# Ten chunks of the convolution's input product in 512- and 256-column multiplications: a two-block transformer kernel on one core

## The chip, the core and the metric

The kernel is one program on one core of a Trainium2 chip. The metric is device time in microseconds (us) for one execution, and the median of several executions counts. Everything is computed from float32 inputs in HBM, and the output is float32.

## The reference, cut to what matters

The reference runs a first model of two layers (short convolution mixer, SwiGLU, dilated attention, SwiGLU) and a hybrid layer behind it, on 256 tokens of width 1024. The change lies in the mixer of the very first layer:

```python
def short_conv_mixer(x, w_in, conv_w, w_out):
    b_gate, c_gate, h = jnp.split(x @ w_in, 3, axis=-1)
    u = c_gate * h
    conv = ...   # depthwise, causal, 3 taps over the tokens: sum over tap of u[t + tap - 2] * conv_w[tap]
    return (b_gate * conv) @ w_out
```

`x` is the RMS-normalised input (256 x 1024), `w_in` is 1024 x 3072, `w_out` is 1024 x 1024.

## The kernel before

**Precision.** Every large product is made of three: a float32 matrix is held as a high part rounded to fp32r and a low part, the rest. The product is high x high + high weights x low input + low weights x high input, all summed in PSUM.

**Chunks.** The weights of all stages come in one sequence of chunks, numbered from the start of the program; a chunk of the stage `conv_in` is 1024 x 256 weights (1 MB, in two halves). `conv_in` has chunks 0 to 11, and `conv_out` chunks 12 to 15. A chunk passes four hands:
- SyncE's queue issues the two loads into `raw` (L583). There are `raw` buffers for two chunks, so the loads of chunk n wait until the low parts of chunk n - 2 are made (`lo_ready`).
- ScalarE copies each half to `w_hi` (L1372), three chunks ahead of the chunk that TensorE is on.
- VectorE subtracts and writes each half to `w_lo` (L1877), two chunks ahead.
- TensorE multiplies. It starts a chunk when both halves of `w_lo` are there (`ready`). `w_hi` and `w_lo` have four slots.

**The product of a chunk.** `feature_major` (L666) makes two output blocks of 128 features x 256 tokens, in one PSUM bank. Each of the 8 k-tiles takes three multiplications of 256 columns: L681 (high weights, high input), L682 (high weights, low input) and L683 (low weights, high input). That is 48 a chunk. Chunk 0 has its own form, and chunk 1 has two short pieces of other work in its middle (`row_and_vectors`).

**What happens with the products.** Chunks come in threes, i = l // 3: first `c_gate`, then `h`, then `b_gate` for 256 features; r = l % 3 tells which. For r = 0 ScalarE copies the bank to `gate` (L1737). For r = 1 VectorE makes `up` = bank x `gate` (L2331), multiplies by the tokens' squared norm factor (L2334, signal `up_set`), and runs the three taps into `cv`: the middle one that all begins with as a scaled copy (L2338, twice), the other two as multiply-adds (L2343, four times), then the norm factor (L2348). For r = 2 VectorE makes `mid` = bank x `cv` (L2358), ScalarE copies it to `a_hi` (L1745) and GpSimd makes `a_lo` (L2514), which `conv_out` reads.

**Order.** Every engine runs an order written by hand, and an engine does its instructions strictly in that order. On VectorE the body for chunk l is: first the low parts of chunk l + 2, then the work on the product of chunk l. At l = 3 it also copies constants out of PSUM and computes the rotary angles (L2351, L1978 to L1990). On ScalarE the body for l is: the high parts of chunk l + 3, then the copy for r = 0, then `a_hi` for r = 2.

The up stage behind already multiplies in another form, `gated_blocks` (L824): `x_hi` and `x_lo` lie side by side in one tile `x_both`, so one multiplication of 512 columns gives high weights x both inputs, and a second of 256 columns adds low weights x high input to the first half. The bank's two halves must then be summed outside TensorE: ScalarE copies the second half out, VectorE adds the first.

Of the kernel before, what the change touches and what calls it, by code (L numbers as in the profile page):

```python
# [25 lines left out]
ALU = mybir.AluOpType  # L26
# [6 lines left out]
T = 256  # L33
# [64 lines left out]
def build(nc, a, out):  # L98
# [4 lines left out]
    with ctx:  # L103
# [173 lines left out]
        by_name = {}  # L277
# [46 lines left out]
        logits_low, logits_set = sem("logits_low"), sem("logits_set")  # L324
        mid_ready = sem("mid_ready")
# [92 lines left out]
        GATE_BANK = (2, 0)  # L418
        NORM_OF = {"up0": 1, "up1": 3}
# [238 lines left out]
        def _(pe):  # L658
# [463 lines left out]
            def emit(ph):  # L1122
                name = ph.name
                if name == "conv_in":
                    for l in range(ph.count):
                        if l > 0:
                            ready(ph, l % 4, l // 4)
                        if l == 0:
                            feature_major_first(ph, 0, x_hi, x_lo, 0)
                        else:  # L1130
                            feature_major(ph, l % 4, x_hi, x_lo, middle=row_and_vectors if l == 1 else None)
# [69 lines left out]
                elif name in ("conv_out", "w_out2"):  # L1201
# [4 lines left out]
                    if name == "conv_out":  # L1206
                        tokens(ph, 0, 0, range(4), bank[0][0], hi, lo, first=True, tile=tile)
# [154 lines left out]
        def _(act):  # L1362
# [364 lines left out]
            def emit(ph):  # L1727
                name = ph.name
                if name == "conv_in":
                    for l in range(ph.count):  # L1730
                        i, r, s = l // 3, l % 3, (ph.n0 + l) % 4
                        ahead(ph, l % 4, l // 4, split, 3)
                        if r == 0:
                            act.wait_ge(product_done, l + 1)
                            if i >= 2:
                                wait_emptied(act, ph, (l - 5) % 4, (l - 5) // 4)
                            nc.scalar.activation(flat2(gate[:, i % 2]), ps[:, s, :], ACT.Copy)\  # L1737
                                .then_inc(emptied[s], 1)
# [4 lines left out]
                        if r == 2:  # L1743
                            wait_emptied(act, ph, l % 4, l // 4)
# [120 lines left out]
        def _(dve):  # L1865
# [451 lines left out]
            def emit(ph):  # L2317
                name = ph.name
                if name == "conv_in":
                    for l in range(ph.count):  # L2320
                        i, r, s = l // 3, l % 3, (ph.n0 + l) % 4
                        ahead(ph, l % 4, l // 4, split, 2)
                        if l == 1:
                            set_row(0)
                            link(nc.vector.tensor_tensor(r_sq[:], rstd[:], rstd[:], ALU.mult))
                        if r == 1:
                            wait_emptied(dve, ph, (l - 1) % 4, (l - 1) // 4)
                            dve.wait_ge(product_done, l + 1)
                            if i == 0:
                                dve.wait_ge(zeroed, 1)  # L2330
                            nc.vector.tensor_tensor(up[:, :, 2:], ps[:, s, :].rearrange("p (m t) -> p m t", m=2),  # L2331
                                                    gate[:, i % 2], ALU.mult).then_inc(emptied[s], 1)
                            wait_emptied(dve, ph, l % 4, l // 4)
# [298 lines left out]
```

## Time and profile before

| | us |
|---|---|
| median of 3 runs | 1077.6 (1077.33 to 1078.9) |
| the profiled execution | 1076.97 |
| its span, first to last instruction | 1074.9 |
| TensorE busy in the span | 1066.9 |
| VectorE busy | 808.1 |
| ScalarE busy | 650.5 |
| GpSimd busy | 55.0 |

The 2.1 us between the execution's time and its span lie before the first and after the last instruction. Matmuls are pipelined: the record of one matmul is longer than the distance to the next one's start, so the distance between starts tells what a row of them costs. A view of a stretch lists groups of like instructions with start, length and count; two independent instructions of VectorE or ScalarE overlap a little at their ends.

### The profile page before, as it was taken

How to read it: one execution, taken by the hardware profiler on the slowest of the kernel's cores; microseconds unless marked ns; L12 is line 12 of the kernel's file. 1: busy time of each engine (PE TensorE's matmuls, PEld its weight loads, DVE VectorE, ACT ScalarE, POOL GpSimd, SP SyncE). 2: the span in 40 equal slices, each digit the busy share in tenths (PEclk: the TensorE clock that was granted, in tenths of full speed). 3: DMA queues.
4: the chain of work that ended last, by engine and by line, in shares of the span. 5: the costliest groups of instructions: out<-in, count | busy, mean ns of one | idle time of the engine just before them, and what ended most of it. 6: DMA issues, size and time to landing. Idle time of an engine off the chain costs nothing.

```text
span 1074.9 us, 19326 instructions
## 1 busy us (share of the span) xinstructions
PE 1066.9 (99%) x7328; PEld 964.1 (90%) x7328; DVE 808.1 (75%) x1227; ACT 650.5 (61%) x982; POOL 55.0 (5%) x47
## 2 busy tenths in 40 slices
PE   8999999999999999999999999999999999999998
PEld 8998888888898999999889888889998989999987
DVE  5986777874588787887878778636797878888960
ACT  6446746564588777777676465535465757656650
POOL 0010000000000000000000000000200111222300
PEclk9999999999999999999999999999999999999999
DMA  8565665678285776552347658753445664565660
GB/s 265 167 206 185 198 214 175 223 250 249 60 236 171 195 193 185 166 160 80 134 146 223 209 164 267 269 158 99 137 135 157 219 206 134 182 194 180 232 235 20
DMA packets 219788, 195.63 MB, mean 182 GB/s; under 512 B 9881, under 2 KB 195277, under 8 KB 219725
## 3 DMA queue, kind: packets, MB, share of 16 engines
q1 hardware_dynamic: 219369, 194.55, 58.1%
q8 instruction: 42, 0.69, 0.3%
q10 hardware_dynamic: 356, 0.22, 0.1%
q14 instruction: 21, 0.17, 0.0%
HBM read 191.85 MB, written 1.05 MB: 179 GB/s over the span
## 4 chain that ended last, share of the span: by engine, by line
PE 90%; DVE 5%; ACT 2%; DMA 1%; issue 1%; SPq 0%; DVEq 0%; ACTq 0%
PE ps L835 24%; PE ps L906 9%; PE ps L736 8%; PE ps L738 8%; PE ps L737 8%; PE ps L681 6%; PE ps L683 6%; PE ps L682 6%; DVE w_lo L1877 2%; PE ps L850 2%; PE ps L849 2%; PE ps L848 2%; DMA raw<-in_conv_w_in 1%; ACT w_hi L1372 1%; PE ps L784 1%; PE ps L750 1%
## 5 line engine op out<-in xcount | busy, mean ns | idle before, releaser
L1877 DVE TENSOR_TENSOR w_lo<-raw,w_hi 128x1024 fp32r<-128x1024 f32 (+1 forms) x298 | 398.2, 1379 | 55.2 <-ACT w_hi L1372 54.2
L1372 ACT ACTIVATE w_hi<-raw 128x1024 fp32r<-128x1024 f32 (+1 forms) x298 | 331.6, 1156 | 117.3 <-PE ps L738 38.2
L835 PE MATMUL ps<-x_both,w_hi 128*128 128x512 f32 x736 | 173.3, 391 | 0.1
L835 PEld LDWEIGHTS ps<-x_both,w_hi 128*128 128x128 f32 x736 | 136.2, 188 | 29.5 <-issue 1.2
L681 PE MATMUL ps<-x_both,w_hi 128*128 128x256 f32 x560 | 159.3, 284 | 0.6 <-DVE w_lo L1877 0.6
L683 PE MATMUL ps<-x_both,w_lo 128*128 128x256 f32 x560 | 158.5, 283 | 0.0
L682 PE MATMUL ps<-x_both,w_hi 128*128 128x256 f32 x560 | 158.5, 283 | 0.0
L736 PE MATMUL ps<-w_hi,a_hi 128*128 128x512 f32 x296 | 115.7, 391 | 0.0
L738 PE MATMUL ps<-w_hi,a_lo 128*128 128x512 f32 x296 | 115.2, 389 | 0.0
L737 PE MATMUL ps<-w_lo,a_hi 128*128 128x512 f32 x296 | 115.2, 389 | 0.0
L681 PEld LDWEIGHTS ps<-x_both,w_hi 128*128 128x128 f32 x560 | 107.5, 192 | 1.4 <-DVE w_lo L1877 1.0
L682 PEld LDWEIGHTS ps<-x_both,w_hi 128*128 128x128 f32 x560 | 107.5, 192 | 0.0
L683 PEld LDWEIGHTS ps<-x_both,w_lo 128*128 128x128 f32 x560 | 107.5, 192 | 0.0
L835 PEld LDWEIGHTS ps<-x_both,w_lo 128*128 128x128 f32 x736 | 91.8, 192 | 2.0
L835 PE MATMUL ps<-x_both,w_lo 128*128 128x256 f32 x736 | 92.8, 283 | 0.0
L1509 ACT ACTIVATE gu<-ps 128x512 f32<-128x512 f32 x20 | 12.0, 598 | 89.2 <-PE ps L835 89.2
L738 PEld LDWEIGHTS ps<-w_hi,a_lo 128*128 128x128 f32 x296 | 55.6, 188 | 11.6
L737 PEld LDWEIGHTS ps<-w_lo,a_hi 128*128 128x128 f32 x296 | 55.6, 188 | 11.3
L736 PEld LDWEIGHTS ps<-w_hi,a_hi 128*128 128x128 f32 x296 | 55.6, 188 | 11.2
L1610 ACT ACTIVATE rot_x<-rot_s 32x512 f32<-32x512 f32 x84 | 52.9, 630 | 16.3 <-DVE rot_s L2123 15.6
L848 PE MATMUL ps<-w_hi,x_both 128*128 128x384 f32 x168 | 56.3, 335 | 0.0
L850 PE MATMUL ps<-w_hi,x_both 128*128 128x384 f32 x168 | 56.2, 335 | 0.0
(263 smaller groups left out, 1698.0 us busy)
## 6 DMA issues: line engine op xcount, KB each, us to landing
raw<-in_ffn_w_gate_up SPq DMA_DIRECT2D x80, 512.0 KB, 5.2
raw<-in_w_up SPq DMA_DIRECT2D x44, 512.0 KB, 4.5
raw<-in_ffn_w_down SPq DMA_DIRECT2D x24, 768.0 KB, 5.9
raw<-in_conv_w_in SPq DMA_DIRECT2D x24, 512.0 KB, 4.9
raw<-in_w_q SPq DMA_DIRECT2D x48, 256.0 KB, 4.7
raw<-in_w_kv SPq DMA_DIRECT2D x48, 256.0 KB, 4.3
raw_v<-in_w_kv SPq DMA_DIRECT2D x48, 256.0 KB, 3.9
raw<-in_w_in SPq DMA_DIRECT2D x20, 512.0 KB, 4.9
```

Of the source, the lines that this page charges most:

```text
L681: nc.tensor.matmul(o, wh[:, k0 + k, c], hi[:, k, :], start=(k == 0), stop=False)
L682: nc.tensor.matmul(o, wh[:, k0 + k, c], low, start=False, stop=False)
L683: ins = nc.tensor.matmul(o, wl[:, k0 + k, c], hi[:, k, :], start=False, stop=(k == kt - 1))
L736: nc.tensor.matmul(o, high, wh[:, k, :], start=(first and k == ks[0]), **flags)
L737: nc.tensor.matmul(o, high, wl[:, k, :], start=False, **flags)
L738: ins = nc.tensor.matmul(o, low, wh[:, k, :], start=False, **flags)
L835: ins = nc.tensor.matmul(o_, w[:, k, c], x, start=(k == 0 and part == int(low_first)), stop=(k == KD - 1), skip_group_check=True)
L848: nc.tensor.matmul(o, high, wh[:, k, :], start=(k == 0), stop=False)
L850: ins = nc.tensor.matmul(o, low, wh[:, k, :], start=False, stop=(k == KD - 1))
L906: ins = nc.tensor.matmul(o_, w[:, k, c], x, start=(k == 0 and part == int(low_first)), stop=(k == KD - 1), skip_group_check=True)
L1372: nc.scalar.activation(w_hi[:, s, a * ph.cols:b * ph.cols], src, ACT.Copy)\
L1877: nc.vector.tensor_tensor(w_lo[:, s, c], src, w_hi[:, s, c], ALU.subtract)\
```

## The change

In `conv_in`, from chunk 2 on:
- TensorE uses `gated_blocks`: 16 multiplications of 512 columns and 16 of 256 a chunk in place of 48 of 256. The two blocks take two PSUM banks; four pairs of banks are used in turn (`CONV_BANK`). In odd chunks the low weights go first. There are extra waits before chunks 2, 3 and 5 and before `conv_out` for the banks.
- ScalarE now first waits for the product of chunk l, copies the second halves of its two banks to `gate`, `up` or `mid` (a 128 x 512 copy, ten of them; three took the place of the copies for r = 0, L1737), and only then makes the high parts of chunk l + 3.
- VectorE adds the first halves in place (ten sums), and for r = 1 and r = 2 the multiplication by `gate` or `cv` comes as an instruction of its own behind the sum, from SBUF.
- In all four threes ScalarE makes the middle tap from `up` (two instructions of 128 x 256) behind the high parts of chunk l + 3; VectorE waits for it (`tap_base`) before the other taps.

```diff
@@ TensorE
-                            feature_major(ph, l % 4, x_hi, x_lo, middle=row_and_vectors if l == 1 else None)
+                            gated_blocks(ph, l % 4, (0, 1), CONV_BANK[l % 4], low_first=(l % 2 == 1)).then_inc(product_done, 1)
@@ ScalarE
-                        ahead(ph, l % 4, l // 4, split, 3)
-                        if r == 0:
+                        if l < 2:
+                            ahead(ph, l % 4, l // 4, split, 3)
+                        if l != 1:
                             act.wait_ge(product_done, l + 1)
...
+                        elif l > 1:
...
+                            dst = (gate[:, i % 2], up[:, :, 2:], mid[:, i % 2])[r]
+                            bank = CONV_BANK[l % 4]
+                            nc.scalar.activation(dst, ps[:, bank:bank + 2, T:2 * T], ACT.Copy).then_inc(conv_low, 1)
+                            ahead(ph, l % 4, l // 4, split, 3)
+                        if r == 1:
+                            act.wait_ge(up_set, i + 1)
+                            for m in range(2):
+                                ins = nc.scalar.activation(cv[:, m, :], up[:, m, 2:], ACT.Identity,
+                                                           scale=v("conv_w", 16 + 2 * i + m))
+                            ins.then_inc(tap_base, 1)
@@ VectorE
+                        if l > 1:
+                            dst = (gate[:, i % 2], up[:, :, 2:], mid[:, i % 2])[r]
+                            bank = CONV_BANK[l % 4]
+                            dve.wait_ge(conv_low, l - 1)
+                            nc.vector.tensor_tensor(dst, ps[:, bank:bank + 2, 0:T], dst, ALU.add).then_inc(emptied[s], 1)
                         if r == 1:
...
+                                link(nc.vector.tensor_tensor(up[:, :, 2:], up[:, :, 2:], gate[:, i % 2], ALU.mult))
                             nc.vector.tensor_tensor(up[:, :, 2:], up[:, :, 2:], by_token(r_sq), ALU.mult)\
                                 .then_inc(up_set, 1)
                             dve.wait_ge(up_set, i + 1)
-                            for m in range(2):
-                                ins = nc.vector.tensor_scalar(cv[:, m, :], up[:, m, 2:], v("conv_w", 16 + 2 * i + m),
-                                                              None, ALU.mult)
-                            link(ins)
+                            dve.wait_ge(tap_base, i + 1)
...
                         if r == 2:
...
-                            nc.vector.tensor_tensor(flat2(mid[:, i % 2]), ps[:, s, :], flat2(cv[:]), ALU.mult)\
-                                .then_inc(emptied[s], 1)
+                            wait_emptied(dve, ph, l % 4, l // 4)
+                            nc.vector.tensor_tensor(mid[:, i % 2], mid[:, i % 2], cv[:], ALU.mult).then_inc(conv_mixed, 1)
```

On VectorE, the work for l = 4 and the start of l = 5, in the kernel before (`hi_ready` is ScalarE's signal for a high half, `v_seq` VectorE's own, `emptied` and `product_done` those of the banks and of TensorE):

```order
L1877 TENSOR_TENSOR w_lo<-raw,w_hi 128x1024 [waits hi_ready] x2
L2331 TENSOR_TENSOR up<-ps,gate 128x2x256 [waits product_done,emptied3]
L2334 TENSOR_TENSOR up<-up,r_sq 128x2x256 [waits emptied0]
L2338 TENSOR_SCALAR cv<-up,vec 128x256 [waits up_set]
L2338 TENSOR_SCALAR cv<-up,vec 128x256
L2343 SCALAR_TENSOR_TENSOR cv<-up,vec,cv 128x256 [waits v_seq]
```

The same place in the changed kernel:

```order
L1906 TENSOR_TENSOR w_lo<-raw,w_hi 128x1024 [waits hi_ready] x2
L2359 TENSOR_TENSOR up<-ps,up 128x2x256 [waits conv_low]
L2370 TENSOR_TENSOR up<-up,gate 128x2x256 [waits emptied0,emptied3]
L2371 TENSOR_TENSOR up<-up,r_sq 128x2x256 [waits v_seq]
L2377 SCALAR_TENSOR_TENSOR cv<-up,vec,cv 128x256 [waits tap_base,up_set]
```

A sum stands ahead of the multiplication by `gate`, and the two scaled copies are gone, with a wait for ScalarE in their place.

On ScalarE, l = 2 to l = 4 in the kernel before:

```order
L1372 ACTIVATE w_hi<-raw 128x1024 [waits product_done,raw_in2]
L1372 ACTIVATE w_hi<-raw 128x1024 [waits raw_in3]
L1745 ACTIVATE a_hi<-mid 128x512 [waits emptied2]
L1372 ACTIVATE w_hi<-raw 128x1024 [waits product_done,raw_in0]
L1372 ACTIVATE w_hi<-raw 128x1024 [waits raw_in1]
L1737 ACTIVATE gate<-ps 128x512 [waits product_done]
```

The changed kernel, from the copy for l = 3 to the one for l = 5:

```order
L1760 ACTIVATE gate<-ps 128x512 [waits product_done]
L1385 ACTIVATE w_hi<-raw 128x1024 [waits product_done,raw_in0]
L1385 ACTIVATE w_hi<-raw 128x1024 [waits raw_in1]
L1760 ACTIVATE up<-ps 128x2x256 [waits conv_mixed,product_done]
L1385 ACTIVATE w_hi<-raw 128x1024 [waits product_done,raw_in2]
L1385 ACTIVATE w_hi<-raw 128x1024 [waits raw_in3]
L1765 ACTIVATE cv<-up,vec 128x256 [waits up_set]
L1765 ACTIVATE cv<-up,vec 128x256
L1760 ACTIVATE mid<-ps 128x512 [waits product_done]
```

The copy of a product now stands ahead of the high parts of the chunk three further on, and the two instructions of the middle tap stand behind those high parts, which wait for the loads (`raw_in`).

## Rows read from the trace of the kernel before

**Rows 1.** The page: engines' busy time and share, granted TensorE clock in 40 slices.
```profile
PE 1066.9 (99%) x7328; PEld 964.1 (90%) x7328; DVE 808.1 (75%) x1227; ACT 650.5 (61%) x982; POOL 55.0 (5%) x47
PEclk9999999999999999999999999999999999999999
```

**Rows 2.** TensorE's waits, whole span: for whom, us in total, times, longest.
```profile
PE ps L698 <- ACT w_hi L1372: 1.5, 1, 1.5
...
PE ps L681 <- DVE w_lo L1877: 0.6, 2, 0.4
```

**Rows 3.** Busy us of PE, PEld, DVE, ACT, POOL (and clock, DMA) in two stretches.
```profile
24.90:51.60 26.70, 26.40 (x221) 26.20 (x219) 25.84 (x44) 12.35 (x14) 1.53 (x1) 1.00 0.51 162
51.60:80.60 29.00, 28.89 (x240) 28.89 (x241) 24.03 (x32) 14.04 (x17) 3.61 (x2) 1.00 0.65 210
```

**Rows 4.** The chain that ended last, 20 to 82 us: start, us, what.
```profile
23.50 1.07 ACT w_hi L1372
24.59 1.23 DVE w_lo L1877
...
31.30 2.36 DVE w_lo L1877 x2
...
34.27 3.36 DVE w_lo L1877 x2
...
49.30 2.37 DVE w_lo L1877 x2
```

**Rows 5.** TensorE's timeline, first matmuls of chunk 7 and of chunk 12.
```profile
51.71 0.39 PE L681 MATMUL ps<-x_both,w_hi 128*128 128x256 f32 x1 [0.41 <-DVE w_lo L1877]
...
80.61 0.40 PE L736 MATMUL ps<-w_hi,a_hi 128*128 128x512 f32 x1
```

**Rows 6.** TensorE's timeline in the up stage, where `gated_blocks` already runs.
```profile
146.59 7.44 PE L835 MATMUL ps<-x_both,w_hi 128*128 128x512 f32 x32
153.87 4.00 PE L835 MATMUL ps<-x_both,w_lo 128*128 128x256 f32 x32
157.71 7.44 PE L835 MATMUL ps<-x_both,w_hi 128*128 128x512 f32 x32
```

**Rows 7.** VectorE's timeline, l = 4 to l = 6.
```profile
44.65 0.68 DVE L2331 TENSOR_TENSOR up<-ps,gate 128x512 f32<-128x512 f32 x1
45.37 0.69 DVE L2334 TENSOR_TENSOR up<-up,r_sq 128x512 f32<-128x512 f32 x1
46.09 0.62 DVE L2338 TENSOR_SCALAR cv<-up,vec 128x256 f32<-128x256 f32 x2
46.74 1.80 DVE L2343 SCALAR_TENSOR_TENSOR cv<-up,vec,cv 128x256 f32<-128x256 f32 x4
...
51.58 0.68 DVE L2358 TENSOR_TENSOR mid<-ps,cv 128x512 f32<-128x512 f32 x1
52.18 2.35 DVE L1877 TENSOR_TENSOR w_lo<-raw,w_hi 128x1024 fp32r<-128x1024 f32 x2
```

**Rows 8.** VectorE's groups in the up stage: busy, mean ns, idle before.
```profile
L2016 DVE TENSOR_TENSOR gu<-gu,rstd 128x512 f32<-128x512 f32 x20 | 13.8, 692 | 0.7
...
L2014 DVE TENSOR_TENSOR gu<-ps,gu 128x512 f32<-128x512 f32 x20 | 13.8, 691 | 40.1 <-ACT gu L1509 40.1
```

**Rows 9.** ScalarE's timeline: 128x256 instructions with a column as scale, bias, or both.
```profile
6.29 1.57 ACT L1387 ACTIVATE x_both<-ps,vec 128x256 fp32r<-128x256 f32 x4 [2.44 <-DVE vec L1965]
...
845.94 1.69 ACT L1724 ACTIVATE gates<-gates,vec 128x256 f32<-128x256 f32 x4
...
949.64 1.10 ACT L1563 ACTIVATE gate<-scaled,vec 128x256 f32<-128x256 f32 x2 [2.24 <-DVE scaled L2062]
```

**Rows 10.** ScalarE's second high half of chunk 10, VectorE's second low half of chunk 9.
```profile
60.41 1.06 ACT L1372 ACTIVATE w_hi<-raw 128x1024 fp32r<-128x1024 f32 x1 [0.32 <-DMA raw<-in_conv_w_in]
...
57.67 1.22 DVE L1877 TENSOR_TENSOR w_lo<-raw,w_hi 128x1024 fp32r<-128x1024 f32 x1 [0.90 <-ACT w_hi L1372]
```

**Rows 11.** The page's DMA issues: count, size, median us from issue to landing.
```profile
raw<-in_conv_w_in SPq DMA_DIRECT2D x24, 512.0 KB, 4.9
```

More of the change, by code:

```diff
@@ L1127, in emit @@
                             ready(ph, l % 4, l // 4)
+                        if l == 2:
+                            pe.wait_ge(vec_set, 1)
+                        elif l == 3:
+                            wait_emptied(pe, ph, 0, 0)
+                            wait_emptied(pe, ph, 1, 0)
+                        elif l == 5:
+                            pe.wait_ge(vec_set, 2)
                         if l == 0:
                             feature_major_first(ph, 0, x_hi, x_lo, 0)
+                        elif l == 1:
+                            feature_major(ph, l % 4, x_hi, x_lo, middle=row_and_vectors)
                         else:
-                            feature_major(ph, l % 4, x_hi, x_lo, middle=row_and_vectors if l == 1 else None)
+                            gated_blocks(ph, l % 4, (0, 1), CONV_BANK[l % 4], low_first=(l % 2 == 1)).then_inc(product_done, 1)
                 elif name in ("up0", "up1"):
@@ L1206, in emit @@
                     if name == "conv_out":
+                        wait_emptied(pe, by_name["conv_in"], 1, 2)
+                        wait_emptied(pe, by_name["conv_in"], 0, 2)
                         tokens(ph, 0, 0, range(4), bank[0][0], hi, lo, first=True, tile=tile)
@@ L1731, in emit @@
                         i, r, s = l // 3, l % 3, (ph.n0 + l) % 4
-                        ahead(ph, l % 4, l // 4, split, 3)
-                        if r == 0:
+                        if l < 2:
+                            ahead(ph, l % 4, l // 4, split, 3)
+                        if l != 1:
                             act.wait_ge(product_done, l + 1)
-                            if i >= 2:
-                                wait_emptied(act, ph, (l - 5) % 4, (l - 5) // 4)
-                            nc.scalar.activation(flat2(gate[:, i % 2]), ps[:, s, :], ACT.Copy)\
-                                .then_inc(emptied[s], 1)
+                        if l == 0:
+                            nc.scalar.activation(flat2(gate[:, 0]), ps[:, s, :], ACT.Copy).then_inc(emptied[s], 1)
+                        elif l > 1:
+                            if r == 0 and i >= 2:
+                                act.wait_ge(up_set, i - 1)
+                            elif r == 1:
+                                act.wait_ge(conv_mixed, i)
+                            elif r == 2 and i >= 2:
+                                act.wait_ge(mid_split, i - 1)
+                            dst = (gate[:, i % 2], up[:, :, 2:], mid[:, i % 2])[r]
[8 more added lines that the diff above has]
+                            ins.then_inc(tap_base, 1)
                         if l == 5:
```

18 lines of the change are left out of this document (9 added, 9 removed).

## The prediction

> **What bounds the kernel now.** I read the page first. TensorE is busy 1066.9 us, 99% of the span, and the granted clock is full in all 40 slices [rows 1]. What the kernel gains or loses is therefore read from TensorE's own pace and from its few waits. The waits come next. Behind its first chunk TensorE stands still almost nowhere: 0.6 us in all for VectorE's low parts in `conv_in` [rows 2]. This would say that VectorE, with 75% of the span, has room. The stretches say otherwise: from 24.9 to 51.6 us VectorE is busy 25.84 of 26.7 us, while TensorE is busy for nearly all of it too [rows 3]. Both engines are full there, side by side. The chain shows which of them leads: from 24.6 us on it runs through VectorE alone, by way of the low parts of chunks 4 and 5, the angles and the taps, up to the low parts of chunk 7 (49.30, 2.37 us long) [rows 4]. TensorE takes them up at 51.71 after 0.41 us of standing still [rows 5]. After that point VectorE is ahead: busy 24.03 of 29.0 us from 51.6 on [rows 3], and TensorE runs chunks 7 to 11 without a stop until 80.61 [rows 5].
>
> So there are two places. Until chunk 7 begins, VectorE's order sets the time, and a faster TensorE only waits longer. From chunk 7 to chunk 11 TensorE sets it.
>
> **TensorE's part.** Before, five chunks take 80.61 - 51.71 = 28.90 us, 5.78 each [rows 5]. The new form stands in the up stage: 32 multiplications of 512 columns take 153.87 - 146.59 = 7.28 us from start to start, 32 of 256 take 157.71 - 153.87 = 3.84 us, so two chunks take 11.12 and one 5.56 us [rows 6]. The change gives 0.22 us a chunk. All ten chunks would give 2.2 us, but only the five from chunk 7 on lie where TensorE sets the time: 5 x 0.22 = **1.10 us gained**. The five before it (2 to 6) only make TensorE arrive 1.1 us earlier at a chunk whose low parts aren't there. The loads have no part in this: ten chunks are the same bytes as before.
>
> **VectorE's part, up to the low parts of chunk 7.** Everything here is in the line that TensorE waits for, since VectorE has 0.9 us of idle time in 26.7 [rows 3].
> - A 128 x 512 sum with one operand in PSUM took 691 ns, a multiplication with both in SBUF 692 [rows 8]. From start to start such an instruction takes 45.37 - 44.65 = 0.72 us where the next one needs its result, and 52.18 - 51.58 = 0.60 where it doesn't [rows 7]. I take these.
> - l = 2: the sum for `mid` with the multiplication behind it, where one instruction stood: +0.72. l = 3: the sum for `gate`: +0.60. l = 4: the sum for `up`: +0.72.
> - The middle tap at l = 1 and l = 4 leaves VectorE, where it took 46.74 - 46.09 = 0.65 us [rows 7]. But nothing is there to fill its place: `up` must be ready before, the other taps need it, and VectorE works in order. ScalarE's pair has no like in the trace. Four instructions of that size from PSUM took 1.57 us, half of which is 0.79; four from SBUF with one column operand took 1.69, half of which is 0.85; a pair from SBUF with two column operands took 1.10 [rows 9]. The second of these has the same source and the same number of columns. A pair overlaps only once where four overlap three times, so I take 0.90. With 0.03 us for the way to the other engine (24.59 against 23.50 + 1.07 in [rows 4]), twice, VectorE stands for 0.96 us in place of 0.65: +0.31, and from +0.2 to +0.5 by the other rows. Twice: **+0.62**.
> - Sum: 0.72 + 0.60 + 0.72 + 0.62 = **2.66 us**, between 2.2 (0.60 for each sum, +0.2 for each tap) and 3.1.
>
> What VectorE waits for must be there. At l = 1 `up` is ready near 28.1 (31.30 - 2.56 for the taps - 0.65), and ScalarE has the tap and the copy of product 2 to do from there, while VectorE comes to that copy at 31.30 + 2.36 = 33.7 [rows 4]. At l = 4 ScalarE must be through with chunk 7's high parts when `up` is ready, at 46.09 + 0.72 + 0.60 + 0.72 + 0.31 = 48.4 [rows 7]. It is busy 12.35 of 26.7 us in this stretch [rows 3], and VectorE's line before has no gap for a high part. The seven more copies of ScalarE cost nothing here for the same reason. GpSimd's first `a_lo` (1.53 us in [rows 3]) lies beside the low parts of chunk 5, which took 3.36 us in place of 2.36 [rows 4]; it moves with them and adds nothing new.
>
> Chunk 7 then begins at 51.71 + 2.66 = 54.37, and `conv_out` at 54.37 + 5 x 5.56 = 82.17, against 80.61: **+1.56 us**.
>
> The Trainium skill (VectorE: DVE Perf Modes, "The TRN2 errata — SBUF-src ops pay a fixed extra latency per instruction") lists 58 cycles of fixed cost for VectorE with its source in SBUF and 120 with it in PSUM. By that table the two multiplications of the line that now read SBUF alone would each be about 0.065 us shorter (an estimate from the page), and the sum 1.43 in place of 1.56. The rows show 692 and 691 ns, no difference, and I keep 1.56.
>
> **Behind chunk 7.** The delay must not grow. The thin place is l = 7. The low parts of chunk 8 were done at 52.18 + 2.35 = 54.5 [rows 7]; they come 2.66 + 0.72 later, at 57.9, since the multiplication of l = 5 waits for its sum too. ScalarE's second high half of chunk 10 ended at 60.41 + 1.06 = 61.47, having waited for its load [rows 10], and the load waits for those low parts. It moves by 3.4 to 64.9, and the middle tap stands behind it on ScalarE: done near 65.8. VectorE would have wanted it at about 63.65 (chunk 9's low parts at 57.67 + 1.22 + 2.66 = 61.5, and three instructions of 0.72, [rows 10]). The other taps take 49.30 - 46.74 = 2.56 [rows 4, 7], chunk 10's low parts 2.3: done at 70.7. TensorE wants chunk 10 at 54.37 + 3 x 5.56 = 71.05. That is 0.4 us of room, and if GpSimd's second `a_lo` costs chunk 8's low parts the 1.0 us that the first one cost, the room is gone and 0.6 us are lost. I take 0.2 for it. Chunk 13 repeats this at l = 10 with the same kind of wait, with some 0.5 us of room.
>
> The sum is +1.56 + 0.2 = **+1.8 us**. On the profiled execution that is 1076.97 + 1.8 = 1078.8. That execution is 0.6 below the median of the runs, and the prediction is for the median: 1077.6 + 1.8 = **1079.4**.
>
> **Rivals.**
> 1. **ScalarE's order becomes the bound a second time (slower).** Place: the tap at l = 7 and l = 10, behind high parts that wait for loads. For it: 0.4 us of room. Against it: that load came 60.41 - 54.5 = 5.9 us after its release, where the median is 4.9 [rows 11]; at the median the room is 1.4 us. It decides when the second high half of chunk 10 ends later than 65.3. Each us later goes whole into the end. With the GpSimd overlap (0.6) and one us more between l = 7 and l = 10: 1.56 + 1.6 = +3.2, 1080.8; with both places bad, +5.
> 2. **TensorE keeps its whole gain (faster).** This needs that VectorE's line wasn't what held chunk 7. Then 10 x 0.22 = 2.2 us and the 0.4 of standing still are the most to be had: 1075.2. The 25.84 of 26.7 us speak against it. Halfway, with VectorE's line 2.2 us longer, it is 2.2 - 1.10 = +1.1, 1078.7, which is still my forecast's case.
> 3. **The clock falls.** TensorE will stand still for about 0.5, 1.2 and 2.4 us before chunks 5, 6 and 7. The longest stop in the trace is 1.5 us [rows 2], and the granted clock stayed at full, 2.4 GHz [rows 1]. No row here is at the lower level. At half the pace each chunk costs 5.6 us more, so one chunk gives 1079.4 + 5.6 = 1085. The Trainium skill (TensorE: Matmul & The Clock Gate, "Part 1: The HAM clock gate") says that an idle TensorE is put back to 1.2 GHz. No run here shows a stop long enough to test it.
>
> **How the numbers follow.** Forecast, VectorE's line lengthened by 2.2 to 3.1 us and little lost behind (+1.0 to +2.4): 0.55. Rival 1 (+2.4 to +5): 0.29. Rival 2: 0.05. Rival 3: 0.03. Less lengthened than I sum, for a reason that I don't see (-1 to +1.0): 0.08. A measurement of this kernel tells 0.2% from no change, 2.15 us: faster is below 1075.4, slower above 1079.8. The forecast lies close to the upper bound, so a fifth of it goes to slower: 0.11 + 0.29 + 0.03, less a little of rival 1 near the bound, makes 0.42; faster 0.05; same 0.53. The range is 1077.4 to 1082.2: below it lie rival 2 and part of the unseen, above it rival 3 and the end of rival 1.
>
> **What would show it.** In the changed trace: 512- and 256-column matmuls at 0.2275 and 0.12 us from start to start, 5.56 us a chunk. TensorE's waits for low parts at chunks 5 to 7 near 4 us in sum, against 0.6. The low parts of chunk 7 done near 54.2, VectorE without idle time before but for two gaps of some 0.96 us ahead of the taps. `conv_out` beginning near 82.2 to 82.4. From there to the end every stage with its old length. Wrong would be: chunk 7 starting before 53.9 or after 54.9, a gap ahead of the taps that is over 2.5 us at l = 7, a wait of TensorE at chunks 10 or 13 over 0.6 us, or a lower granted clock.

## The result, and the profile after

The changed kernel takes 1080.59 us (median of 17 runs, 1078.11 to 1081.59), the kernel before 1077.6 on the same chip (17 runs). The ratio is 1.0024, 95% interval 1.0018 to 1.0031: 2.6 to 3.0 us slower. The forecast was 1079.4 with a range of 1077.4 to 1082.2, a chance of 0.53 for no difference that can be told and 0.42 for slower by over 0.2%. The range holds the time, and the less likely of the two came. The forecast itself is 1.2 us too low. In the profiled execution one thing explains what it missed, and a second profile, further down, shows that it isn't the only one.

The profiled execution took 1080.59 us, its span is 1078.2. Its page beside [rows 1]:

```profile
PE 1068.5 (99%) x7168; PEld 959.5 (89%) x7168; DVE 813.1 (75%) x1229; ACT 657.0 (61%) x997; POOL 54.5 (5%) x47
...
PEclk8999999999999999999999999999999999999999
```

There are 160 matmuls fewer, as the change says (ten chunks, 32 in place of 48), and VectorE and ScalarE have more to do. The first slice is not at full clock any more. TensorE's waits, beside [rows 2] (for whom, us in total, times, longest):

```profile
PE ps L873 <- DMA h<-in_x: 2.1, 2, 1.9
...
PE ps L837 <- DVE w_lo L1906: 1.8, 1, 1.8
```

The wait for low parts is 1.8 us, where it was 0.6, and it is one single stop. TensorE's timeline from chunk 2 to `conv_out`, beside [rows 5] (start, length, line, form, count, in brackets the standing still before it):

```profile
24.77 3.82 PE L837 MATMUL ps<-x_both,w_hi 128*128 128x512 f32 x16
...
54.57 2.74 PE L837 MATMUL ps<-x_both,w_lo 128*128 128x256 f32 x16 [1.84 <-DVE w_lo L1906]
57.11 8.48 PE L837 MATMUL ps<-x_both,w_hi 128*128 128x512 f32 x32
65.43 4.00 PE L837 MATMUL ps<-x_both,w_lo 128*128 128x256 f32 x32
...
84.03 0.39 PE L738 MATMUL ps<-w_hi,a_hi 128*128 128x512 f32 x1
```

Chunk 7 begins at 54.57 (forecast 54.37), `conv_out` at 84.03 (forecast 82.2 to 82.4; before 80.61). From `conv_out` to the end of the span it is 1078.2 - 84.03 = 994.2 us, before 1074.9 - 80.61 = 994.3. So the whole loss lies ahead of `conv_out`: 3.42 us, of which 54.57 - 51.71 = 2.86 are there when chunk 7 begins, and 0.56 come behind it. That second part should have been a gain of 1.1. From start to start, the 16 multiplications of 256 columns at 54.57 take 2.54 us and not 1.92, and the 32 of 512 behind them 8.32 and not 7.28. Together they take 1.66 us too long, and 1.66 - 1.10 = 0.56. Why, the stretches show, beside [rows 3] (busy time of PE, PEld, DVE, ACT, POOL, then the granted clock, DMA share and GB/s):

```profile
0.00:20.00 20.00, 16.23 (x94) 15.11 (x95) 8.75 (x16) 11.95 (x21) 0.51 (x6) 0.83 0.81 257
...
52.00:56.00 4.00, 2.15 (x18) 1.95 (x17) 3.93 (x6) 2.40 (x5) 0.00 (x0) 0.99 0.36 95
56.00:59.00 3.00, 3.00 (x12) 2.61 (x11) 3.00 (x2) 2.05 (x3) 1.54 (x1) 0.50 0.89 268
59.00:61.00 2.00, 2.00 (x10) 1.60 (x9) 2.00 (x4) 1.06 (x1) 0.00 (x0) 0.92 0.79 224
```

TensorE stood still for 1.84 us, worked again from 54.57 on, and from 56 to about 59.3 us it was granted 0.50, which is 1.2 in place of 2.4 GHz. That is some 3.3 us at half the pace, which accounts for the 1.66 us. The first 20 us are at 0.83 too. There TensorE had stood still for 1.9 us for the input's load (L873). Whether that made the clock fall isn't shown: in the trace of the filled stop, further down, it stood still for 1.49 and 1.51 us within the first 12 us and stayed at full clock. This earlier fall cost next to nothing here, since until chunk 7 VectorE sets the time, and its first `up` begins at 26.53, where it began at 26.64 before.

VectorE's line, beside [rows 7], and ScalarE's pair for the tap at l = 4:

```profile
46.24 0.68 DVE L2359 TENSOR_TENSOR up<-ps,up 128x512 f32<-128x512 f32 x1
47.03 0.69 DVE L2370 TENSOR_TENSOR up<-up,gate 128x512 f32<-128x512 f32 x1
47.76 0.69 DVE L2371 TENSOR_TENSOR up<-up,r_sq 128x512 f32<-128x512 f32 x1
49.51 1.89 DVE L2377 SCALAR_TENSOR_TENSOR cv<-up,vec,cv 128x256 f32<-128x256 f32 x4 [1.06 <-ACT cv L1765]
51.42 0.69 DVE L2382 TENSOR_TENSOR cv<-cv,rstd 128x512 f32<-128x512 f32 x1
52.15 2.36 DVE L1906 TENSOR_TENSOR w_lo<-raw,w_hi 128x1024 fp32r<-128x1024 f32 x2
54.43 0.68 DVE L2359 TENSOR_TENSOR mid<-ps,mid 128x512 f32<-128x512 f32 x1
```

```profile
48.48 0.91 ACT L1765 ACTIVATE cv<-up,vec 128x256 f32<-128x256 f32 x2 [4.34 <-DVE up L2371]
```

I measure this line from the start of the first `up` (l = 1) to the instruction behind the low parts of chunk 7. That is a length on one engine, so an early or late start of the program doesn't enter. Before it is 51.58 - 26.64 = 24.94 us, after it is 54.43 - 26.53 = 27.90: **+2.96**, forecast +2.66.

### The profile page after: what moved, and what is told of

The parts are those of the page before. It is cut to its first block, busy times and chain, and to the rows that moved or that the text cites. A ratio compares the mean times of both kernels' runs of the same rounds, so it can differ in the third digit from the quotient of the medians.

```text
span 1078.2 us, 19030 instructions
## 1 busy us (share of the span) xinstructions
PE 1068.5 (99%) x7168; PEld 959.5 (89%) x7168; DVE 813.1 (75%) x1229; ACT 657.0 (61%) x997; POOL 54.5 (5%) x47
## 3 DMA queue, kind: packets, MB, share of 16 engines
HBM read 191.85 MB, written 1.05 MB: 179 GB/s over the span
## 4 chain that ended last, share of the span: by engine, by line
PE 88%; DVE 6%; ACT 2%; DMA 2%; SPq 1%; issue 1%; DVEq 0%; ACTq 0%
PE ps L837 27%; PE ps L908 9%; PE ps L738 8%; PE ps L739 8%; PE ps L740 8%; PE ps L683 5%; PE ps L685 5%; PE ps L684 5%; DVE w_lo L1906 3%; PE ps L852 2%; PE ps L851 2%; PE ps L850 2%; DMA raw<-in_conv_w_in 1%; ACT w_hi L1385 1%; PE ps L951 1%
## 5 line engine op out<-in xcount | busy, mean ns | idle before, releaser
L837 PE MATMUL ps<-x_both,w_hi 128*128 128x512 f32 x896 | 211.5, 392 | 0.0
L837 PEld LDWEIGHTS ps<-x_both,w_hi 128*128 128x128 f32 x896 | 166.8, 189 | 35.2 <-DVE w_lo L1906 0.7
L837 PEld LDWEIGHTS ps<-x_both,w_lo 128*128 128x128 f32 x896 | 112.2, 192 | 4.5 <-DVE w_lo L1906 2.0
L837 PE MATMUL ps<-x_both,w_lo 128*128 128x256 f32 x896 | 113.6, 284 | 1.8 <-DVE w_lo L1906 1.8
L683 PE MATMUL ps<-x_both,w_hi 128*128 128x256 f32 x400 | 113.8, 284 | 0.0
L685 PE MATMUL ps<-x_both,w_lo 128*128 128x256 f32 x400 | 113.2, 283 | 0.0
L684 PE MATMUL ps<-x_both,w_hi 128*128 128x256 f32 x400 | 113.2, 283 | 0.0
L683 PEld LDWEIGHTS ps<-x_both,w_hi 128*128 128x128 f32 x400 | 76.8, 192 | 0.3 <-issue 0.3
L684 PEld LDWEIGHTS ps<-x_both,w_hi 128*128 128x128 f32 x400 | 76.8, 192 | 0.0
L685 PEld LDWEIGHTS ps<-x_both,w_lo 128*128 128x128 f32 x400 | 76.7, 192 | 0.0
```

What stands on the lines that cost most here:

```text
L683: nc.tensor.matmul(o, wh[:, k0 + k, c], hi[:, k, :], start=(k == 0), stop=False)
L684: nc.tensor.matmul(o, wh[:, k0 + k, c], low, start=False, stop=False)
L685: ins = nc.tensor.matmul(o, wl[:, k0 + k, c], hi[:, k, :], start=False, stop=(k == kt - 1))
L837: ins = nc.tensor.matmul(o_, w[:, k, c], x, start=(k == 0 and part == int(low_first)), stop=(k == KD - 1), skip_group_check=True)
```

## Experiments

**The theory**: VectorE's line up to chunk 7 is longer by the three sums and the two taps, and its end decides when TensorE takes up chunk 7. Behind that, the new form gains 1.1 us; and the stop before chunk 7 sometimes lets the clock fall, which costs about 1.6 us. **Rivals**: the low clock comes from something else (the late load, chance) and the stop has no part in it; the loss is from ScalarE's new order; the angles alone are what makes chunk 7 late, so that elsewhere VectorE has room.

### The tap put back

```diff
@@ ScalarE
-                        if r == 1:
-                            act.wait_ge(up_set, i + 1)
-                            for m in range(2):
-                                ins = nc.scalar.activation(cv[:, m, :], up[:, m, 2:], ACT.Identity,
-                                                           scale=v("conv_w", 16 + 2 * i + m))
-                            ins.then_inc(tap_base, 1)
@@ VectorE
-                            dve.wait_ge(tap_base, i + 1)
+                            for m in range(2):
+                                ins = nc.vector.tensor_scalar(cv[:, m, :], up[:, m, 2:], v("conv_w", 16 + 2 * i + m),
+                                                              None, ALU.mult)
+                            link(ins)
```

> The changed kernel with the middle tap back on VectorE. Theory A: the two gaps ahead of the taps (1.74 and 1.75 us from the start of the multiplication by r_sq to the first tap, against 1.38 and 1.37 before) go, chunk 7 begins 0.75 us earlier, near 53.8: 1080.6 - 0.75 = 1079.8 if the clock still falls, 1078.4 if a stop of 1.1 us no longer lets it fall. If the move to ScalarE relieved VectorE, as a count of busy time says (0.6 us an instance), it would be slower, 1081.8.

1079.16 us against 1077.08 for the kernel before, ratio 1.0014 (1.0005 to 1.0024). The line is 53.65 - 26.57 = 27.08 us: 2.14 of the 2.96 are the sums, and 0.82 are the two taps. The stops stay:

```profile
46.06 3.96 PE L837 MATMUL ps<-x_both,w_hi 128*128 128x512 f32 x16 [0.72 <-DVE w_lo L1900]
...
53.79 2.17 PE L837 MATMUL ps<-x_both,w_lo 128*128 128x256 f32 x16 [1.86 <-DVE w_lo L1900]
```

In this execution the clock stayed full behind a stop of 1.86 us. So such a stop doesn't lower it each time. The other executions have both of the cases that were expected: the 4 with a mean clock of 1.00 have a median of 1077.94 (expected 1078.4), the 7 below it 1079.58 (expected 1079.8). In those 7 no trace shows where the clock fell.

### The tap moved alone

The kernel before, with nothing but the middle tap on ScalarE (the lines of the diff above, the other way round).

> The kernel before with the middle tap on ScalarE and nothing else. Theory A: VectorE stands 0.37 to 0.41 us longer at each tap than its own two instructions took, so the line up to chunk 7 is 25.7 us in place of 24.94 and the time rises by 0.75. If the offload frees VectorE, the line shortens by up to 1.2 us and the 0.4 us stop goes: 0.4 faster.

The line is 52.97 - 27.30 = 25.67 us, +0.73. The two gaps ahead of the taps:

```profile
29.77 1.79 DVE L2347 SCALAR_TENSOR_TENSOR cv<-up,vec,cv 128x256 f32<-128x256 f32 x4 [1.05 <-ACT cv L1743]
...
48.14 1.80 DVE L2347 SCALAR_TENSOR_TENSOR cv<-up,vec,cv 128x256 f32<-128x256 f32 x4 [1.06 <-ACT cv L1743]
```

VectorE stands for 1.05 us in place of working 0.65. The time is 1077.86 against 1077.43, ratio 1.0003 (0.9994 to 1.0011), which alone is no difference that can be told. In executions at full clock it is 1077.85 (10 runs) against 1077.20 (26 runs), +0.65, and with so few runs that isn't clear of noise either. What is shown is the line: taking work off VectorE made it longer.

### The sums cut short

```diff
-                            nc.vector.tensor_tensor(dst, ps[:, bank:bank + 2, 0:T], dst, ALU.add).then_inc(emptied[s], 1)
+                            w = 8 if l < 5 else T
+                            nc.vector.tensor_tensor(dst[:, :, 0:w], ps[:, bank:bank + 2, 0:w], dst[:, :, 0:w], ALU.add)\
+                                .then_inc(emptied[s], 1)
```

The sums for l = 2 to 4 are made for 8 of 256 tokens only; the rest of these products lacks its first half.

> The changed kernel with VectorE's sums at l = 2, 3 and 4 made for 8 of 256 columns only, so part of the convolution's input product is left incomplete. Theory A: each sum still costs its start, 0.15 to 0.25 us of 0.60 to 0.79, so the line up to chunk 7 is about 1.5 us shorter than the changed kernel's 27.9, near 26.4, and chunk 7 begins 1.5 us earlier: 1.2 to 1.5 us under the changed kernel's median with a full clock, and 2 to 3 under its median if the shorter stop (0.3 us) no longer lets the clock fall: near 1077.9. Rival D: no effect.

The time is 1078.85 against 1077.43, ratio 1.0016 (1.0007 to 1.0025), 0.9 above what was expected. The short sums take 0.17 us each, but the line is 53.25 - 25.94 = 27.31 us, only 0.59 less than the changed kernel's. Two things of opposite sign are in this. From start to start the three sums take 0.20, 0.08 and 0.27 us in place of 0.72, 0.60 and 0.79, which is 1.56 less, as expected. But at l = 1 VectorE waited 2.00 us for the tap and not 1.04, which is 0.96 more: ScalarE's high part ahead of the tap had waited for its load. TensorE now stops in three places:

```profile
34.33 3.93 PE L837 MATMUL ps<-x_both,w_hi 128*128 128x512 f32 x16 [0.58 <-DVE w_lo L1906]
...
53.39 2.18 PE L837 MATMUL ps<-x_both,w_lo 128*128 128x256 f32 x16 [1.85 <-DVE w_lo L1906]
...
71.36 3.92 PE L837 MATMUL ps<-x_both,w_hi 128*128 128x512 f32 x16 [1.03 <-DVE w_lo L1906]
```

The last one, before chunk 10, is a new place, and it is the place of the prediction's rival 1. The load for ScalarE's second high part of chunk 10 came late, the tap stands behind that high part, and VectorE waited 3.37 us for it at l = 7:

```profile
64.43 1.06 ACT L1385 ACTIVATE w_hi<-raw 128x1024 fp32r<-128x1024 f32 x1 [3.13 <-DMA raw<-in_conv_w_in]
...
66.39 1.80 DVE L2379 SCALAR_TENSOR_TENSOR cv<-up,vec,cv 128x256 f32<-128x256 f32 x4 [3.37 <-ACT cv L1765]
```

### The angles later

```diff
@@ VectorE (angles() stood under l == 3; its last five instructions are angles_end)
+                        if l == 6:
                             angles()
+                        if l == 9:
+                            angles_end()
```

ScalarE's two table instructions move from l = 5 to l = 10 with it.

> The changed kernel with the rotary angles (4.5 us of VectorE, 39.47 to 43.97 in its trace) moved from l = 3 to l = 6 and l = 9, and ScalarE's sine and cosine from l = 5 to l = 10. Theory A (VectorE's line up to chunk 7 sets the time): chunk 7's low parts come at 49.9 in place of 54.4, TensorE no longer stops in front of it, the ten chunks give their whole 2.2 us and the 0.4 us of the old stop: near 1075.1, and conv_out begins some 5.5 us earlier than in the changed kernel when the start is alike. Theory B (the clock falls because TensorE stops in front of chunk 7): the granted clock stays full from 50 us on. Rival C (the fall of the clock belongs to the new form of multiplication or to the program's start, not to the stop): a stretch at 0.5 is still there between 50 and 62 us. Rival D (the new form costs time somewhere else): stays above 1077.6.

A miss. It takes 1078.04 against 1077.08, ratio 1.0009 (1.0000 to 1.0018), and 1075.1 was expected. The line up to chunk 7 is 4.25 us shorter (51.29 - 27.64 = 23.65). But the stops only went elsewhere:

```profile
35.08 3.93 PE L837 MATMUL ps<-x_both,w_hi 128*128 128x512 f32 x16 [0.79 <-DVE w_lo L1906]
69.96 3.92 PE L837 MATMUL ps<-x_both,w_hi 128*128 128x512 f32 x16 [1.11 <-DVE w_lo L1906]
87.27 0.50 PE L738 MATMUL ps<-w_hi,a_hi 128*128 128x512 f32 x1 [0.47 <-DVE w_lo L1906]
```

And over the whole stage:

```profile
27.00:81.00 54.00, 52.09 (x302) 45.54 (x301) 49.19 (x68) 30.49 (x40) 4.65 (x3) 1.00 0.56 175
```

VectorE is busy for 49.19 of 54.0 us, and three gaps ahead of the taps (1.05, 1.39, 1.06) are another 3.5. That leaves 1.3 us. With the sums and the handed-over taps VectorE has next to no room anywhere in `conv_in`, and where the angles stand decides in which chunk that is seen. "The angles alone make chunk 7 late" falls.

The half of the forecast that is about the clock held: no stop is longer than 1.11 us, the clock is full in the whole stage, and no execution has a mean below 0.997. The four that have 0.997 take 1078.18, the other seven 1078.04.

### The new form from chunk 7 on only

Chunks 2 to 6 as before; chunks 7 to 11 in the new form, with the tap on VectorE.

```diff
@@ TensorE
+                        elif l < 7:
+                            feature_major(ph, l % 4, x_hi, x_lo, bank=4 if l == 5 else None)
                         else:
                             gated_blocks(ph, l % 4, (0, 1), CONV_BANK[l % 4], low_first=(l % 2 == 1)).then_inc(product_done, 1)
@@ VectorE
-                        if l > 1:
+                        if l >= 7:
```

A first form of it left chunk 5 in its old bank, which is one of the pair that chunk 7 takes.

> The new form of multiplication, the copies and the sums only from chunk 7 on, chunks 2 to 6 and the middle tap as in the kernel before. Theory A: VectorE's line up to chunk 7 is that of the kernel before, so the stop there stays at 0.4 us and conv_out begins 1.1 us earlier than before: 1076.5, clock full. Rival D (the new form costs time where it stands): not faster than 1077.6.

1076.97 against 1077.08, ratio 0.9999 (0.9990 to 1.0008). The mistake shows as a stop before chunk 7:

```profile
53.29 2.14 PE L837 MATMUL ps<-x_both,w_lo 128*128 128x256 f32 x16 [1.27 <-DVE mid L2396]
```

With chunk 5 in bank 4, which is the form of the diff:

> As e3_from_seven, but chunk 5 keeps its old form in bank 4, so that chunk 7 (banks 0 and 1) needn't wait for VectorE's work on chunk 5; in e3_from_seven that wait was 1.27 us in place of 0.4. Theory A: chunk 7 begins right behind its low parts, line from the first up to the low parts of chunk 7 24.95 us as before, TensorE gains 5 x 0.22: 1.1 us under the kernel before, 0.9 under e3_from_seven. Rival D (the new form itself costs time): no better than e3_from_seven.

1076.25 against 1077.43, ratio 0.9989 (0.9980 to 0.9997): 1.2 us faster, where five chunks at 0.22 make 1.1. In the trace the five chunks take 27.80 us (52.36 to 80.16), 5.56 each. VectorE's line keeps its old length, 50.48 - 25.53 = 24.95. So the gain behind chunk 7 is real and of the size forecast, and it is the sums and taps ahead of chunk 7 that cost.

### The form from chunk 4 on, with the angles later

Both halves of what was learned: the old form for chunks 2 and 3, the new one from 4 on, the tap on VectorE, and the angles at l = 6 and l = 9.

> New form from chunk 4 on, middle tap on VectorE, rotary angles at l = 6 and l = 9, sine and cosine at l = 10. Theory A: up to chunk 7 VectorE gives away 4.5 us of angles and takes on 2.0 us of sums, so its line is 2.4 us shorter than before and TensorE stops nowhere in front of chunks 5 to 13: eight chunks give 1.8 us and the old stop, where it stands, up to 0.4: 1.8 to 2.2 us under the kernel before. If VectorE is full again behind chunk 7 (sums and angles, 3.4 + 4.5 us against 5.0 of idle time), TensorE stops in front of chunk 10 or 13 and the gain is 1 us or less.

**1075.91** against 1077.4, ratio 0.9985 (0.9976 to 0.9994). At full clock it is 1075.07 (6 runs) against 1077.34 (17 runs), 2.3 us less. The two engines side by side, and the one wait for low parts that is left:

```profile
27.00:78.00 51.00, 51.00 (x315) 46.03 (x314) 48.94 (x70) 27.14 (x33) 4.64 (x3) 1.00 0.56 177
```

```profile
PE ps L683 <- DVE w_lo L1910: 0.2, 1, 0.2
```

TensorE is busy for all of 51 us, and VectorE still has 2 us. Eight chunks at 0.22 are 1.8, and the old standing still before chunk 7 is gone as well. By its median it is the fastest kernel of this study. Which of its two steps gives how much wasn't run apart.

### The clock: work in the long stop

TensorE gets 14 multiplications of 256 columns, into a bank whose content isn't needed any more, ahead of its wait for chunk 7.

```diff
+                        if l == 7:
+                            pe.wait_ge(emptied[3], used[7])
+                            pe.wait_ge(hi_ready, ph.n2(3, 1) + 2)
+                            for _ in range(14):
+                                nc.tensor.matmul(ps[:, 0, 0:T], slot(w_hi, 3, ph)[:, 0, 0:P], x_hi[:, 0, :], start=True,
+                                                 stop=True, skip_group_check=True)
```

> The changed kernel with 14 multiplications of 256 columns (0.12 us each, 1.7 us) between chunk 6 and chunk 7, into a bank that chunk 7 overwrites. They lie in TensorE's stop of 1.84 us. Theory B: the clock stays at full behind chunk 7, the 1.66 us that chunks 7 and 8 lose in the changed kernel's trace (2.54 for 1.92 and 8.32 for 7.28) are not lost, and the median falls to the level of the changed kernel's executions with a full clock, 1079.4. Rival C: clock falls all the same, 1080.6. Chunk 7's low parts come at the same time in both.

1079.53 against 1077.08, ratio 1.0023 (1.0013 to 1.0033). The line has its length of the changed kernel (54.91 - 26.96 = 27.95). Since 1.0023 can't be told from 1.0024, I ran the changed kernel and this one again, beside each other on one chip:

> The changed kernel as it is, on the same chip as the others of this set: +2.5 to +3 us against the kernel before, and in about half of the executions a second fall of the clock behind 50 us.

> The changed kernel with 14 multiplications in TensorE's stop in front of chunk 7, as e4_filled_wait, beside the changed kernel on the same chip. Theory B: under the changed kernel by the share of executions in which its clock falls, about half of 1.5 us, and no execution with a mean clock under 0.997. Rival C: the same time and the same clocks as the changed kernel.

The changed kernel took 1080.56 (7 runs, ratio 1.0030, 1.0018 to 1.0041), the filled one 1079.26 (11 runs, 1.0020, 1.0011 to 1.0029). The medians differ by 1.3 us. The intervals of the two ratios overlap, but five of the 7 executions of the changed kernel are slower than all 11 of the filled one. One part of the expectation failed: one filled execution has a mean clock of 0.996, below the 0.997 that was to be the lowest. The profiled execution of the changed kernel is a lesson of its own:

```profile
46.88 3.94 PE L837 MATMUL ps<-x_both,w_hi 128*128 128x512 f32 x16 [0.87 <-DVE w_lo L1906]
...
55.07 2.17 PE L837 MATMUL ps<-x_both,w_lo 128*128 128x256 f32 x16 [2.34 <-DVE w_lo L1906]
...
72.37 3.96 PE L837 MATMUL ps<-x_both,w_hi 128*128 128x512 f32 x16 [0.36 <-DVE w_lo L1906]
...
83.66 0.39 PE L738 MATMUL ps<-w_hi,a_hi 128*128 128x512 f32 x1
```

```profile
57.00:58.00 1.00, 1.00 (x7) 0.83 (x6) 1.00 (x2) 0.67 (x3) 0.92 (x1) 1.00 0.97 271
58.00:59.00 1.00, 1.00 (x6) 0.83 (x5) 1.00 (x1) 0.89 (x1) 0.63 (x1) 1.00 0.69 231
```

Here TensorE started earlier (chunk 2 at 23.02), and the same lateness of VectorE falls into the stops that I had forecast: 0.87 before chunk 6 and 2.34 before chunk 7, 0.36 before chunk 10. The clock didn't fall, and chunk 7 to `conv_out` took 28.59 us where the other execution needed 29.46. Even so that is 0.79 more than five chunks at 5.56: 0.36 is the stop before chunk 10, and 0.43 more lies around the two stops (the 16 multiplications of 256 columns behind the first take 2.01 and not 1.92 us, the 16 of 512 behind the second 3.80 and not 3.64, and 0.18 are ahead of it). A stop costs more than its standing still. The stop before chunk 10 follows a late tap at l = 7, rival 1's place again:

```profile
67.39 1.80 DVE L2377 SCALAR_TENSOR_TENSOR cv<-up,vec,cv 128x256 f32<-128x256 f32 x4 [2.69 <-ACT cv L1765]
```

In the filled kernel the stop is cut in two:

```profile
52.08 1.84 PE L1132 MATMUL ps<-x_both,w_hi 128*128 128x256 f32 x14
54.59 2.17 PE L837 MATMUL ps<-x_both,w_lo 128*128 128x256 f32 x16 [0.68 <-DVE w_lo L1912]
```

All runs of the two kernels, by the mean granted clock of the execution, say what the single profile can't:

| | runs | full clock | median of these | below full | median of these |
|---|---|---|---|---|---|
| changed kernel, two series | 24 | 10 | 1079.41 | 14 | 1080.81 |
| filled, two series | 20 | 14 | 1079.41 | 6 | 1079.36 |
| kernel before, three chips | 86 | 65 | 1077.02 | 21 | 1078.19 |

At full clock the two are equal, 1079.41. Below it the changed kernel is 1.4 us slower and the filled one isn't. A mean doesn't say where the clock fell, but the traces show what makes which. About 6.8 us at half clock within the first 20 us give 0.997 (the tap moved alone, 0.83 up to 20 us). About 3.4 us at half clock give 0.998, be they at the start or behind a stop; both kinds come below. In the changed kernel's first profile a fall at the start and one behind the stop give 0.995. That mean, the lowest of all, comes in 8 of the 24 runs of the changed kernel and in none of the 20 of the filled one or the 86 of before. (Once each it also came with the sums cut short and in the last experiment below, which both have a stop of 1.85 us or more.) The other 6 runs below full are at 0.998, with a median of 1080.81, so there the fall behind the stop is likely but not shown.

What a fall at the start costs must be kept apart. In the kernel before, whose trace has no long stop, the runs below full are 1.2 us slower. With the angles later it was 0.1 (1078.18 against 1078.04), and the filled kernel's six are not slower as a group, though its three at 0.997 take 1079.63 to 1080.00. There VectorE's line is the later one and covers most of it. So most of the 1.4 us belongs to the stop.

### The clock: stops in the kernel before

If the stop is the cause, the old form must show it too. Two variants of the kernel before, in which VectorE multiplies into a tile that nobody reads: four times at l = 3, and five times at l = 4.

```diff
@@ first variant, behind angles() at l = 3
+                            for _ in range(4):
+                                link(nc.vector.tensor_tensor(acc[:], up[:, :, 2:], cv[:], ALU.mult))
@@ second variant, behind the taps of l = 4
+                        if l == 4:
+                            for _ in range(5):
+                                link(nc.vector.tensor_tensor(acc[:], up[:, :, 2:], cv[:], ALU.mult))
```

> The kernel before with four more VectorE multiplications of 128 x 512 (0.72 us each, 2.9 us) behind the angles, written to a tile that nobody reads. Theory A: the whole of it is in the line that TensorE waits for, 2.9 us slower. Theory B: TensorE's stop in front of chunks 6 and 7 grows to 3.3 us in sum with the old form of multiplication, the clock falls to 0.5 for some us in many executions, and the median is 4 to 5 us above the kernel before. Rival C (the fall belongs to the new form): clock stays full behind 50 us, +2.9 alone.

1079.5 against 1077.43, ratio 1.0020 (1.0010 to 1.0030). The delay is spread over two stops, none over 0.92 us, and behind them the clock is full; this execution's mean of 0.998 comes from a fall at the start:

```profile
47.66 0.39 PE L681 MATMUL ps<-x_both,w_hi 128*128 128x256 f32 x1 [0.68 <-DVE w_lo L1877]
...
54.60 0.38 PE L681 MATMUL ps<-x_both,w_hi 128*128 128x256 f32 x1 [0.92 <-DVE w_lo L1877]
```

```profile
10.00:20.00 10.00, 9.78 (x69) 9.78 (x70) 7.11 (x11) 8.29 (x16) 0.00 (x0) 0.83 0.88 272
...
50.00:70.00 20.00, 19.08 (x159) 18.88 (x158) 18.16 (x25) 12.14 (x14) 2.41 (x2) 1.00 0.64 207
```

The line is 2.92 us longer, as in the changed kernel, and the median rises by 2.1. I had expected at least the whole 2.9. That VectorE isn't the later one in every execution of the kernel before (TensorE starts later in some) would explain the 0.8; it wasn't tested by itself.

> The kernel before with five more VectorE multiplications of 128 x 512 (3.6 us) at l = 4, between the low parts of chunks 6 and 7, written to a tile that nobody reads. TensorE then stops once, for up to 4.0 us, in front of chunk 7, with the old form of multiplication. Theory B (a stop lets the clock fall): the granted clock falls to 0.5 behind that stop in most executions and the median is 3.2 to 3.6 + 1.5, some 5 us above the kernel before. Rival C (the fall belongs to the new form or the start): clock full behind 50 us, +2.8 to +3.6 only.

1081.91 against 1077.4 (5 runs), ratio 1.0035 (1.0022 to 1.0049): 4.5 us for 3.6 us of added work. The trace:

```profile
56.54 0.39 PE L681 MATMUL ps<-x_both,w_hi 128*128 128x256 f32 x1 [3.57 <-DVE w_lo L1877]
```

```profile
59.00:60.00 1.00, 1.00 (x7) 1.00 (x7) 1.00 (x1) 0.90 (x1) 0.36 (x1) 0.50 0.89 288
60.00:61.00 1.00, 1.00 (x6) 1.00 (x6) 1.00 (x2) 0.00 (x0) 0.00 (x0) 0.50 0.90 294
```

One stop of 3.57 us, and again the clock is at half some 1.6 us after the engine is back at work. Four of its five runs are below full clock; the fifth, at full clock, took 1079.12. The old form does it too, so it isn't the new form that lowers the clock, and not ScalarE's new order.

## Why the prediction came out as it did

- **TensorE's part** is right: 0.2275 and 0.12 us from start to start where it runs at full clock and without a stop, 5.56 us a chunk, and 1.2 us for five chunks alone (forecast 1.10). That the gain ahead of chunk 7 is worth nothing is right too.
- **The sums** are right: 2.14 us against 2.04. Of the 0.10 more, 0.07 is the way from the sum for `up` to the multiplication behind it, 47.03 - 46.24 = 0.79 and not 0.72 (for `mid` it is 34.55 - 33.83 = 0.72).
- **The taps** are mis-sized by a third: 0.82 in the changed kernel, 0.73 alone, against 0.62. ScalarE's pair took 0.91, as forecast (0.90). The two hand-overs took 0.14 and not 0.06: the gap is 1.04 to 1.06 and not 0.96. Why the taps cost 0.09 more in the changed kernel than alone stays open; at l = 4 the four multiply-adds behind the gap took 1.89 us there and 1.80 alone.
- **Chunk 7** was to begin at 54.37 and began at 54.57 and 55.07 in the two traces. In the second, ScalarE was late at l = 1 (a gap of 1.68 ahead of the taps), which I had given no price, and 55.07 is beyond the 54.9 that I had named as a sign of being wrong.
- **Behind chunk 7** the wait at chunk 10 was 0 and 0.36 us; 0.2 had been taken for it. Rival 1's mechanism is real, though small here: the gap ahead of the taps at l = 7 was 1.29 us in the first trace and 2.69 in the second, over the 2.5 that I had named, and with the sums cut short 3.37, with a stop of 1.03 us before chunk 10. What one of its stops costs beyond the standing still, here some 0.3 us, was in no term.
- **The stops** were forecast as 0.5, 1.2 and 2.4. The trace with an early start has 0.87 and 2.34, the one with a late start a single 1.84. How late TensorE itself starts differs from one execution to the next, and I took the start of the one trace that I had.
- **The clock** is the step that failed. Rival 3 named the mechanism and its place, the stop before chunk 7. But I gave it 0.03 where 8 of 24 executions have the mean that only both falls together gave in a trace, and 14 of 24 are below full, against 21 of 86 of the kernel before. And I priced it at 5.6 us, a whole chunk at half the pace, where it was 3.3 us at half the pace: 1.66. I had read [rows 1 and 2] as "1.5 us of standing still and the clock stayed full" and put the limit far above; the trace held no row between 1.5 us and the 2.4 that I forecast, so this chance could not be near zero.

In executions at full clock the changed kernel takes 1079.41. That this is the forecast's 1079.4 is partly luck. The forecast added 1.8 us to 1077.6, a median of executions of which some were below full clock themselves. The kernel before takes 1077.02 at full clock (1076.76 to 1077.34 on the three chips), which makes the change 2.4 us and not 1.8, and in the second trace, at full clock, `conv_out` begins 83.66 - 80.61 = 3.05 us later than before. Of the 1.3 that the sum lacked there, 0.3 are the line, 0.6 the late tap at l = 1, 0.2 the stop before chunk 10 and 0.4 the cost around the stops; the first `up` began 0.24 earlier. The rest, up to 1080.59, comes from executions below full clock, over half of all, at 1.4 us each. What isn't settled is what decides within one kernel: behind a stop of 1.84 us the clock fell in one execution, behind stops of 1.85, 1.86 and 2.34 us it didn't in three others.

## What to carry to other kernels

Where two engines run side by side, a faster form on one of them pays only in those chunks in which that engine is the later one; if it hands work to the other, put it only there (here from chunk 4 or 7 on, not from 2). A step between two steps of the same engine isn't a relief when it goes elsewhere: the engine stands for its length and two hand-overs. And a new stop of TensorE of near 2 us or more has two prices, its own length and some executions at half the clock behind it, so here several short stops were better than one: two of 0.68 and 0.92 us cost 2.1 us for 2.9 us of added work, one of 3.57 us cost 4.5 for 3.6.

## What the hardware showed beyond that

- The clock fell 1.4 to 1.6 us after TensorE was back at work, not in the stop, and stayed at 1.2 GHz for about 3.4 us while the engine was busy without a gap (restart at 54.57 and 0.50 from 55.95 to 59.3; restart at 56.54 and 0.50 from 58.1 to 61.5). The Trainium skill (TensorE: Matmul & The Clock Gate, "Part 1: The HAM clock gate") gives the clock gate two states, 1.2 and 2.4 GHz, and the lower one to an idle engine. Both traces with a fall behind a stop agree on the levels, with 0.50 and 1.00 in all stretches that lie on one side of a switch, and in both the engine had stood still before; the low stretch itself lies on busy time.
- VectorE took longer where GpSimd's `a_lo` ran beside low parts: two low halves took 3.44 us, and 2.35 alone. `a_lo` took 1.54 us there; in the kernel before the second one took 2.06, beside a low half of 1.56 in place of 1.22.

```profile
56.58 1.54 POOL L2545 TENSOR_TENSOR a_lo<-mid,a_hi 128x512 fp32r<-128x512 f32 x1 [19.06 <-ACT a_hi L1774]
```

```profile
55.76 3.44 DVE L1906 TENSOR_TENSOR w_lo<-raw,w_hi 128x1024 fp32r<-128x1024 f32 x2
59.13 0.68 DVE L2359 TENSOR_TENSOR gate<-ps,gate 128x512 f32<-128x512 f32 x1
59.73 2.35 DVE L1906 TENSOR_TENSOR w_lo<-raw,w_hi 128x1024 fp32r<-128x1024 f32 x2
```

- In the changed trace a 128 x 512 sum with one operand in PSUM took 0.68 us and a multiplication with both in SBUF 0.69: no relief for the source in SBUF.
